# Retrieval, gates and expert stages of a two-layer decoder trunk: gates stored in pieces, transposes moved into the next block, products loaded earlier

## The reference, cut to what matters

```python
q = (hc @ wq).reshape(t, 8, 2, 128)               # 512 tokens, 8 heads
s = einsum("thpk,pnk->thpn", q, subkeys)          # two score rows of 128 keys each
s1, i1 = top_k(s[:, :, 0], 16); s2, i2 = top_k(s[:, :, 1], 16)
best, j = top_k((s1[..., :, None] + s2[..., None, :]).reshape(t, 8, 256), 16)
e = i1[j // 16] * 128 + i2[j % 16]                # 16 of 16384 experts per head
gate = softmax(best)
act = gelu(einsum("thkd,td->thk", u_tab[e], hc))
out = einsum("thk,thkd->td", gate * act, v_tab[e])
```

## Time and profile before

| | us |
|---|---|
| median of 3 runs (3141.48 to 3150.63) | 3143.73 |
| profiled execution, its own time | 3141.54 |
| its span, first to last instruction | 3139.8 |
| TensorE busy | 2904.3 (93%) |
| VectorE busy | 2430.9 (77%) |
| GpSimd busy | 1424.9 (45%) |
| ScalarE busy | 1207.3 (38%) |
| DMA, mean | 271 GB/s |

### The profile page before, as it was taken

One profiled execution on the slowest core, in us unless ns is written; L12 is line 12 of the kernel. 1 busy time (PEld: TensorE's weight loads), 2 busy tenths in 40 slices (PEclk: granted clock), 3 DMA queues, 4 the chain that ended last, 5 costly groups with the idle time before them and its releaser, 6 DMA issues.

```text
span 3139.8 us, 50852 instructions
## 1 busy us (share of the span) xinstructions
PE 2904.3 (93%) x15754; PEld 2554.2 (81%) x15754; DVE 2430.9 (77%) x4532; ACT 1207.3 (38%) x1590; POOL 1424.9 (45%) x878
## 2 busy tenths in 40 slices
PE   5888999999998899999899899999999989999997
PEld 3657999989888788888777689989888878888885
DVE  7965679999995688888765307799999937888887
ACT  2333333345553333333333324333555523333332
POOL 2623367776667122222324244777766651222221
PEclk8999999999999999999999899999999989999998
DMA  6336567779898899999935124777788898999996
GB/s 240 134 128 221 199 206 240 242 263 349 308 350 321 301 353 350 355 356 352 351 122 174 66 100 138 229 251 239 277 328 328 310 348 308 352 353 351 357 347 232
DMA packets 352434, 849.74 MB, mean 271 GB/s; under 512 B 30048, under 2 KB 194016, under 8 KB 350176
## 3 DMA queue, kind: packets, MB, share of 16 engines
q1 hardware_dynamic: 239888, 479.53, 44.5%
q0 software_dynamic: 73728, 268.47, 23.6%
q10 hardware_dynamic: 38736, 100.84, 8.1%
HBM read 741.76 MB, written 106.95 MB: 270 GB/s over the span
## 4 chain that ended last, share of the span: by engine, by line
PE 54%; DVE 21%; issue 11%; POOL 7%; DMA 4%; ACT 1%; SPq 0%; POOLq 0%; DVEq 0%; ACTq 0%
PE bank L1418 11%; PE bank L1419 11%; PE bank L1420 11%; POOL w_lo L407 6%; DVE oh_c L995 5%; DVE oh_j L999 5%; PE bank L1360 4%; PE bank L1362 4%; PE bank L1361 4%; DVE rows L1160 2%; PE bank L1260 2%; PE bank L1262 2%; PE bank L1261 2%; DVE oh_i L996 2%; DMA x<-u_rows,u_idx 1%
## 5 line engine op out<-in xcount | busy, mean ns | idle before, releaser
L407 POOL TENSOR_TENSOR w_lo<-w_raw,w_hi 128x1024 fp32r<-128x1024 f32 x338 | 838.6, 2481 | 694.1 <-ACT w_hi L517 692.2
L517 ACT ACTIVATE w_hi<-w_raw 128x1024 fp32r<-128x1024 f32 x594 | 629.1, 1059 | 1346.3 <-PE bank L1420 668.6
L1360 PE MATMUL bank<-h_hi,w_hi 128*128 128x384 f32 x2048 | 702.7, 343 | 42.5 <-POOL w_lo L407 29.8
L1362 PE MATMUL bank<-h_lo,w_hi 128*128 128x384 f32 x2048 | 688.9, 336 | 0.0
L1361 PE MATMUL bank<-h_hi,w_lo 128*128 128x384 f32 x2048 | 688.3, 336 | 0.0
L461 POOL DMA_INDIRECT shared<-stream,v_idx x256 | 246.8, 964 | 830.9 <-DVE rows L1069 746.6
L1418 PE MATMUL bank<-w_hi,h_hi 128*128 128x512 f32 x1536 | 600.7, 391 | 16.6 <-ACT h_hi L642 14.3
L1419 PE MATMUL bank<-w_hi,h_lo 128*128 128x512 f32 x1536 | 600.0, 391 | 0.0
L1420 PE MATMUL bank<-w_lo,h_hi 128*128 128x512 f32 x1536 | 599.8, 390 | 0.0
L1039 DVE TENSOR_TENSOR w_lo<-w_raw,w_hi 128x1024 fp32r<-128x1024 f32 x256 | 313.7, 1226 | 199.9 <-ACT w_hi L517 199.0
L1360 PEld LDWEIGHTS bank<-h_hi,w_hi 128*128 128x128 f32 x2048 | 387.1, 189 | 58.9 <-issue 55.9
(11 more groups left out here) (193 smaller groups left out, 3584.6 us busy)
## 6 DMA issues: line engine op xcount, KB each, us to landing
w_raw<-stream SPq DMA_DIRECT2D x600, 512.0 KB
act_dram<-act_words ACTq DMA_DIRECT2D x256, 192.0 KB
gate_dram<-shared ACTq DMA_DIRECT2D x12, 4096.0 KB, 16.1
act_words<-act_dram SPq DMA_DIRECT2D x256, 192.0 KB
shared<-gate_dram SPq DMA_DIRECT2D x128, 384.0 KB
oh_j<-mod_rows SPq DMA_DIRECT2D x60, 512.0 KB, 4.7
oh_i<-mod_rows SPq DMA_DIRECT2D x20, 512.0 KB, 5.4
shared<-mod_rows SPq DMA_DIRECT2D x16, 512.0 KB, 14.0
```

Source lines behind the costliest of these rows:

```text
L407: nc.gpsimd.tensor_tensor(lo_of(grp, s), w_raw[:, s, :], hi_of(grp, s).bitcast(F32), ALU.subtract).then_inc(S["lo_ready"], 1)
L517: nc.scalar.activation(hi_of(grp, s), w_raw[:, s, :], ACT.Copy).then_inc(S["hi_ready"], 1)
L1360: MM(o, hi, h_hi[:, k, P:T], start=(k == 0), stop=False)
L1362: ins = MM(o, hi, h_lo[:, k, P:T], start=False, stop=(k == KC - 1))
```

## The change

The program of each engine changes, the arithmetic doesn't.

1. Retrieval: TensorE makes the transposes of retrieval b after tile 4 of the next block, not at the end of its own; VectorE copies them out in the middle of the next retrieval (`take_transposed`). Early dots: 30, not 36: none in the first half of retrieval 1; the first set stands before L881 now, the second behind the candidate sums. The fetches move by some tiles. Loops over blocks are written out.
2. Gate groups: `oh_c` and `oh_i` are made by one compare, the three `oh_j` by one multiply. The first six groups get one dot more each.
3. Gate stores: 8 pieces of 512 KB, issued during the next 8 groups; those of the last half one after another.
4. Into V: products have a buffer of their own (`act_v`) and go to columns of `h_hi` and `h_lo` that the U stage doesn't read. So the first loads, product and `w_lo` come before the last U tile.
5. V: the ring of V rows has 8 slots, axpy n goes with tile n, none is left behind the end.

```diff
-V_RING = 4
+V_RING = 8
+GATE_PIECES = 8
-EARLY = 2 * DB * EARLY_SET
+EARLY = (2 * DB - 1) * EARLY_SET
-    return EARLY + g + (g + 1) // 2
+    return EARLY + g + (g + 1) // 2 + min(g, EARLY_SET)
...
+        def product(h, s):
+            return h[:, DB * (s % 2):DB * (s % 2) + DB, 0:P]
...                                             # SP
                 for s in range(2):
+                    load(first - 1, s)
+                for r in range(2):
+                    sp.wait_ge(g_st[r], GATE_STORED * ((l + 1) * DB + 1))
+                for s in range(RING):
+                    sp.wait_ge(act_st[s], 16 * (l * EXPERT_TILES // RING + 1))
+                    load_products(0, s)
+                for s in range(2, RING):
+                    load(first - 1, s)
+                for s in range(RING):
                     load(first, s)
...                                             # GpSimd: U fetches done by tile r of block b
-                        end = 2 * (b - 1) * EARLY_SET + min(max(r - 1, 0), EARLY_SET) + (
-                            EARLY_SET if r == TILES_PER_BLOCK - 1 else max(r - 10, 0))
+                        if b == 1:
+                            end = min(max(r - 2, 0), EARLY_SET)
+                        else:
+                            end = (2 * b - 3) * EARLY_SET + min(r + 1, EARLY_SET) + (
+                                min(r - 6, EARLY_SET) if 7 <= r < 11 else EARLY_SET if r >= 11 else 0)
...                                             # ScalarE
+                pieces = [range(0, 2), range(2, 4), range(4, 5), range(5, 6), range(6, 7), range(7, 8), (), ()]
+                for n in range(2 * DB):
+                    for g in range(HALF // GROUP):
+                        expert_step(at + (n * (HALF // GROUP) + g) // RING, g % RING)
+                        if n:
+                            for piece in pieces[g]:
+                                store_gates(n - 1, piece)
...
+                for piece in range(GATE_PIECES):
+                    store_gates(2 * DB - 1, piece)
...                                             # VectorE
-                    V.tensor_tensor(oh_c[:], keys, of_group(j_t, g), ALU.is_equal).then_inc(S["oh_cmp"], 1)
-                    V.tensor_tensor(oh_i[:, s, :, :, :], keys, of_group(i_t, g), ALU.is_equal)
+                    V.tensor_tensor(oh_ic[:, s:3:2 - s, :, :, :], keys, of_group(keys_t, g), ALU.is_equal
+                                    ).then_inc(S["oh_cmp"], 1)
                     dve.wait_ge(S["oh_cmp"], groups + g + 1)
-                    for w in range(3):
-                        ins = V.tensor_tensor(oh_j[:, s, w, :, :, :], oh_c[:], of_group(gate_p[:, w, :], g), ALU.mult)
-                    ins.then_inc(S["oh_ready"], 1)
+                    V.tensor_tensor(oh_j[:, s, :, :, :, :], oh_c.unsqueeze(1).to_broadcast([P, 3, PAIR, NK, 2]),
+                                    of_group(gate_p, g), ALU.mult).then_inc(S["oh_ready"], 1)
...
+                gated(0, 0, True)
+                gated(0, 1, True)
                 dve.wait_ge(S["lo_ready"], first)
                 w_low(0, 0)
...
+                for s in range(2 * RING):
+                    two_ahead(s // RING, s % RING, 2 * RING)
+                    axpy(s)
...                                             # TensorE
+                for b in range(TB + 1):
+                    at = b * per
+                    for s in range(RING):
+                        experts(at, s, banked + at * RING + s)
+                    if b >= 2:
+                        transposed(b - 1)
+                    if b < TB:
+                        with pe.Fori(1, per) as r:
+                            for s in range(RING):
+                                experts(r + at, s, r * RING + (banked + at * RING + s))
```

More of the change, by code:

```diff
@@ L354, in _ @@
                 sp.dma_start(x_dram, x[:]).then_inc(S["x_st"], 16)
-                with sp.Fori(u_first + 1, first) as i:
+                with sp.Fori(u_first + 1, first - 1) as i:
                     for s in range(RING):
@@ L861, in retrieve, with dot @@
-                def retrieve(b, plus, fetched):
+                def dot(n):
+                    r = n % U_RING
+                    dve.wait_ge(u_ld[r], 16 * (l * len(range(r, SLOTS, U_RING)) + n // U_RING + 1))
+                    V.scalar_tensor_tensor(out=u_row(n), in0=u_row(n), scalar=1.0, in1=rows[:], op0=ALU.mult,
+                                           op1=ALU.mult, accum_out=dots[:, n:n + 1]).then_inc(S["dot"], 1)
+                def early_dots(b, half):
+                    done = 2 * b - 3 + half
+                    for n in range(max(done, 0) * EARLY_SET, (done + 1) * EARLY_SET):
+                        dot(n)
@@ L879, in retrieve @@
                     then_top(ins)
+                    if not fetched:
+                        early_dots(b, 0)
                     for hp in range(2 * HEADS):
@@ L1080, in peer_dve @@
-                V.tensor_tensor(dots[:], dots[:], gate_0[:], ALU.mult).then_inc(S["weight"], 1)
-                dve.wait_ge(S["weight"], l + 1)
-                products(1, True)
-                with dve.Fori(2, last) as i:
-                    products(i)
-                for s in range(RING):
-                    two_ahead(last, s)
-                    axpy(last, s)
-                for s in range(RING):
-                    axpy(last + 1, s)
+                for s in range(2 * RING):
+                    two_ahead(s // RING, s % RING, 2 * RING)
+                    axpy(s)
@@ L1090, in peer_dve @@
+                with dve.Fori(1, (last - 1) // 2) as i:
+                    for s in range(2 * RING):
+                        two_ahead(i * 2 + s // RING, s % RING, 2 * RING)
+                        axpy(s, i * V_RING)
+                for i in (last - 1, last):
+                    for s in range(RING):
+                        two_ahead(i, s, 2 * RING if i < last else RING)
+                        axpy(i * RING + s)
                 dve.wait_ge(S["axpy"], (l + 1) * SLOTS)
@@ L1363, in experts, with transposed @@
                     ins.then_inc(S["tile_done"], 1)
[L1365 to L1371 removed]
+                def transposed(b):
                     pe.wait_ge(S["tr_read"], b + l * DB)
```

196 lines of the change are left out of this document (85 added, 111 removed).

## The result

The changed kernel takes 3155.72 us (median of 9 runs, 3152.53 to 3165.26), the kernel before 3147.38 us (9 runs, 3139.04 to 3152.91): ratio 1.0035, 95% interval 1.0020 to 1.0049. It is slower by 0.35%; the forecast was 3102 us, and the range 3062 to 3129 does not hold the time. The profiled execution took 3159.8 us with a span of 3158.0, against 3141.5 and 3139.8 before. The two profiles are thus 18 us apart and the medians 8: one profile is one draw, and runs of either kernel differ by 13 to 14 us. A possible reason for a part of that came out in the ninth experiment. What follows splits up the 18 us of the profiles, so it explains where time goes within a layer better than it explains the 0.35%.

A forecast was written before the change was run, and what follows sets the result against it. A third of the wait chain was V's matmuls, with TensorE full there and VectorE nearly full in the groups. Terms -5 + 4 - 8 - 17 - 16 = -42 on 3141.5 gave 3099.5, median 3102 us; 8-in-10 range 3062 to 3129.

The forecast's parts named there:

- 1, retrievals and transposes: Retrievals and last transposes: VectorE gains nothing, TensorE a little; -2 us in layer 0, -3 in layer 1, -5 in all.
- tile 68: Sign at the first group after the retrievals: right if tile 68 starts within 5 us of 661.
- The wait of VectorE: Sign at the last transposes: a VectorE wait on them over 15 us would show the forecast wrong.
- 2, groups: Gate groups with merged one-hots and six added dots: 12.35 us per pair; +5 and -1 us by layer, +4 in all.
- groups get ahead: Rival, gate groups: VectorE's compare precedes `w_lo`, ending the 6.2 us cadence; -27 in one layer (3075), both 3047; chance 12%.
- 3, gate stores: Last U tiles from 116: stores in pieces end the long fetch stall; -4.6 and -3.7 us, -8; bounds -14 and +3.
- 4, into V: Entry from U to V: first products loaded early, 3 us left per layer; -8.6 and -8.3 us, -17 in all.
- 5, out of V: End of V: eight slots and no axpys left behind, so transposes start earlier; -9.7 and -6.5 us, -16 in all.
- give it back: Rival: picks and double fetches cost 7 us more per layer, V's entry saves 5 in all; 3128 us, chance 12%.
- L1418's first wait: Sign at the first V matmul: right if its wait is under 1 us.
- L1440's place: Sign at V's end: right if L1440 comes within 3 us of the last V matmul.
- the longest fetch: Sign after a gate store: right if no fetch takes over 8 us.

The follow-up runs named there:

- experiment 9: Changed kernel with the exponential later, U-tile weights and second V ring ahead of their waits, and earlier U fetches; last eight pieces still in one row: 3113.49 us, 0.9901.
- Experiment 1: Changed kernel with a retrieval's exponential on ScalarE before tile 15 of its block, not tile 12: 3134.94 us, ratio 0.9982.
- experiment 10: Experiment 8 with the last retrieved block's transposes issued by TensorE two tiles into the ring, not four: 3108.28 us, ratio 0.9863.
- experiment 12: Experiment 9 with the last transposes three tiles in: 3109.42 us, ratio 0.9879.
- experiment 7: Changed kernel with five one-hot instructions of 1024 elements instead of two merged ones, in the new layout: 3165.62 us, ratio 1.0058.
- experiment 13: Experiment 12 with one dot less in each of the first six groups, those dots put after the last group: 3113.35 us, ratio 0.9886.
- experiment 6: Changed kernel with gate stores whole again, one 4 MB store instead of eight pieces: 3162.21 us, ratio 1.0042.
- Experiment 2: Changed kernel with the last eight gate-store pieces issued two per tile over tiles 116 to 119, not in a row: 3161.13 us, ratio 1.0056.
- Experiment 3: Changed kernel with all of the last four U tiles' weights loaded ahead of SyncE's wait for the gate-store pieces: 3146.81 us, ratio 1.0005.
- Experiment 8: Changed kernel with later exponential, last pieces two per tile, U-tile weights and second V ring ahead of their waits, and earlier U fetches: 3117.88 us, ratio 0.9909.
- Experiment 4: Changed kernel with the second ring of V's weights and products loaded ahead of the wait for the last activations: 3151.13 us, ratio 1.0021.
- Experiment 11: Experiment 10 with the first two V tiles' weights loaded ahead of SyncE's wait for the last gate pieces: 3116.96 us, ratio 0.9897.

## Why the prediction was wrong, step by step

The step that failed most is the first; the third and the fourth failed in the same way, on a smaller scale.

**1, retrievals and transposes: the step that failed.** Forecast -5, measured +21.5 in the two layers. VectorE's timing was about right (retrievals forecast to end at 502, 583 and 656, measured 507, 586 and 665). What the step left out is who else waits inside a retrieval. It costed six dots, their fetches, GpSimd and TensorE, and never named ScalarE, whose exp stands in its queue ahead of a tile's `w_hi` and of the Gelu that frees TensorE's output bank. Before, VectorE was early enough, and the trace before has no wait of ScalarE for it. After, ScalarE stands 17.7 us for it in layer 0 (8.9 the longest): the 8 us by which I let a retrieval wait for its fetches, and called that "VectorE gains nothing", TensorE paid for. Experiment 1 shows it: 17 us by the ratios, 21 by the medians, back from that place alone, which is more than the 11 or 8 between the two kernels. The step's other half failed as well: "tile 68 starts at about 661" (675 in fact), and "only then come the last transposes, where VectorE has waited 5 us" was priced at nothing, as TensorE was thought to get to its group only at 673.8. It got there at 679.4 and waited; experiments 10 and 12 put this at 3 to 8 us per layer. The wait of VectorE that the text set as a sign (over 15 us wrong) came to 9.8.

**2, groups.** The pair's cadence was right: 12.35 forecast, 12.43 measured (223.7 / 18), and the merge saved as little as said (experiment 7). The forecast of +5 and -1 came out at +9.1 and +2.7 mostly since I gave the added dots 1 us in all. Three of the first six groups carry three dots, and VectorE is busy 73.6 of the 77 us there, so TensorE waits for it; experiment 13, without the added dots, took 2 to 4 us less than experiment 12. The Trainium skill's rule on the shared port pair (SBUF — State Buffer, "SBUF: two separate sides") agrees with the trace: alone the compare is 1.23 us and beside `w_lo` 2.1 to 3.4. The two ways of experiment 9 agree as well: in one of them GpSimd stands behind VectorE's multiply in every second group, in the other VectorE alone stands. The rival "groups get ahead" was thus real in mechanism and size (-17 for a layer, where I gave -27), but the changed kernel didn't go that way in its profile.

**3, gate stores.** Forecast -8, measured +12.8. That the long fetch goes is right (VectorE waits for a row 8.7 us at most; 18.89 again in experiment 6), though a little over the 8 us that I had set as the sign; and tiles 120 to 123 take 4.6 to 4.8, GpSimd's 4.85. Wrong was "0.35 each" for an issue: a rate taken from single issues far apart, used for eight in a row, where the sum is 9.2. I had put "`w_raw` for tile 126 stands behind the wait" in as the bound of +3; both together made +6.4 per layer. Experiments 2 and 3 show that they cover one another: in tiles 116 to 127, 2 alone gives nothing, 3 alone 8 us per layer, and both (in 8) 12, of which 6 come back at V's entry.

**4, into V.** Forecast -17, measured -8.6. The entry itself is as forecast, TensorE going from U to V without a pause. "Late next is the gate load for tiles 4 and 5", with 3 us left for it, named the right tile and half the price: it is the wait for the last activation's store, moved by the change from ahead of the first products to ahead of the second ring, 4.6 us, 1.7 at the lower clock in the tile behind it, and 0.5 to 0.9 in what follows. Experiment 4 takes it away.

**5, out of V.** Forecast -9.7 and -6.5, measured -10.0 and -6.5. Here nothing else was queued behind what the change moved.

The rival that was right on V's entry and on the retrievals ("give it back", 3128) had 12%, with "picks and double fetches", not with the exp, and it falls 28 us short; slower than before had 8%. Of the signs, L1418's first wait (none) and L1440's place (2.2 us behind) came out; tile 68 (675, not within 5 us of 661), the longest fetch and V's first tiles did not. The chances rested on a list of waits that the change takes away. For each queue that the change made later I had asked what it does, not what is written behind it.

## What to carry to other kernels

When an engine's program grows ahead of a point, list every engine that waits for that point and read what stands behind each wait in its queue; the bill comes from there, not from the engine that got longer. Price an issue by how many stand in a row, not by a single one. And where stages meet, take waits away together and in one profile each: three of the moves here (2, 4 and 11) gave back half or all of their gain at another wait in what follows, and the version that keeps what worked (experiments 10 and 12, 3108 and 3109 us) is 1.2 to 1.4% faster than before.

## What the runs showed of the hardware

- ScalarE's issue of 512 KB stores in 4 KB rows: eight in a row cost 0.34 to 0.52 us for the first three, then 1.3 to 2.0 each, and the engine does nothing else meanwhile. Two behind each tile cost 0.44 to 0.55 each (experiment 2). What the issues wait for, no trace shows.
- Merged `bf16` one-hots keep their rate: 0.68 us for 128 x 1024, 1.23 for 128 x 2048, 1.76 for 128 x 3072, alone; 3.8 for the last with GpSimd's `w_lo` running when it was issued.
- The last of eight 512 KB pieces landed 22.5 to 23.6 us after its issue (experiments 8, 10 and 11, layer 0), where one 4 MB store took 16.1 in the kernel before.
- After TensorE had stood 2.6 to 7.6 us, its next tile ran at a granted clock of 0.70 to 0.73 on the average and took 5.7 to 6.0 us in place of 4.2.
- The group stage has two lasting ways to run with the same instructions, 5.65 and 6.21 us per tile. One profiled layer of 26, in all kernels with the merged one-hots, stayed in the fast one for the whole stage. Experiments 10, 12 and 13 each had one execution 14 to 22 us below the rest of its own, which is what one such layer would give; those executions have no profile. What starts it stays open: in experiment 9 it began after tiles of 8.7 and 6.9 us; in experiment 6 a tile of 13.5 us was followed by 8 groups at 5.6 us in layer 0 and by 16 in layer 1, with slower ones among them; and in 13 a lead given to VectorE did not hold.
